# Down projections of two feed-forward nets with one level of Strassen's scheme on two of three token blocks

## The reference, cut to what matters

```python
def swiglu(x, w_gate, w_up, w_down):
    return (jax.nn.silu(x @ w_gate) * (x @ w_up)) @ w_down

    h = x + 0.5 * swiglu(rmsnorm(x, ffn1_norm), ffn1_w_gate, ffn1_w_up, ffn1_w_down)
    ...
    h = h + 0.5 * swiglu(rmsnorm(h, ffn2_norm), ffn2_w_gate, ffn2_w_up, ffn2_w_down)
```

## Time and profile before

| | us |
|---|---|
| median of 3 runs | 1815.75 (1815.69 to 1816.22) |
| the profiled execution | 1815.54 |
| its span, first to last instruction | 1813.7 |
| TensorE busy | 1795.7 |
| VectorE busy | 1030.8 |
| GpSimd busy | 639.2 |
| ScalarE busy | 597.6 |

### The profile page before, as it was taken

One profiled execution on the slowest core, in us unless ns is written; L12 is line 12 of the kernel. 1 busy time (PEld: TensorE's weight loads), 2 busy tenths in 40 slices (PEclk: granted clock), 3 DMA queues, 4 the chain that ended last, 5 costly groups with the idle time before them and its releaser, 6 DMA issues.

```text
span 1813.7 us, 30511 instructions
## 1 busy us (share of the span) xinstructions
PE 1795.7 (99%) x12169; PEld 1783.0 (98%) x12169; DVE 1030.8 (57%) x1726; ACT 597.6 (33%) x1155; POOL 639.2 (35%) x669
## 2 busy tenths in 40 slices
PE   8999999999999999999999999999999999999998
PEld 7999999999999999999999999999999999999998
DVE  6658755554554554823774768555455455544546
ACT  7411322232323233532112455223233323323324
POOL 2687232332333222203994221233233322323321
PEclk9999999999999999999999999999999999999999
DMA  6132111112111111455114501111212111111112
GB/s 171 36 128 101 46 41 53 53 41 60 41 59 48 47 53 39 143 127 123 47 41 125 154 14 53 53 53 43 62 37 60 47 47 53 47 53 48 53 48 94
DMA packets 162494, 119.68 MB, mean 66 GB/s; under 512 B 10242, under 2 KB 156226, under 8 KB 161844
## 3 DMA queue, kind: packets, MB, share of 16 engines
q1 hardware_dynamic: 157012, 110.36, 20.7%
q0 software_dynamic: 864, 5.28, 0.9%
q10 hardware_dynamic: 4480, 2.10, 0.5%
HBM read 102.01 MB, written 15.72 MB: 65 GB/s over the span
## 4 chain that ended last, share of the span: by engine, by line
PE 96%; DVE 2%; ACT 1%; issue 0%; POOL 0%; DVEq 0%; POOLq 0%
PE bank_pair L1004 21%; PE bank_pair L1006 21%; PE bank_pair L1005 21%; PE bank_down L1004 10%; PE bank_down L1006 10%; PE bank_down L1005 10%; DVE HT L2104 1%; DVE XL L2127 1%; PE bank_pair L1387 0%; PE bank_pair L1360 0%; PE bank_pair L1480 0%; PE bank_pair L1379 0%; PE bank_pair L1112 0%; DVE S L2121 0%; PE bank_down L1154 0%
## 5 line engine op out<-in xcount | busy, mean ns | idle before, releaser
L2329 DVE SCALAR_TENSOR_TENSOR HT<-bank_down,HT 128x344 f32<-128x344 f32 (+2 forms) x480 | 246.3, 515 | 369.1 <-PE bank_down L1006 367.1
L1004 PE MATMUL bank_down<-HH,DQH 128*128 128x344 f32 (+2 forms) x924 | 296.0, 320 | 0.0
L1005 PE MATMUL bank_down<-HL,DQH 128*128 128x344 f32 (+2 forms) x924 | 295.0, 319 | 0.0
L1004 PE MATMUL bank_pair<-XHM,U_hi 128*128 128x344 f32 x720 | 230.5, 320 | 1.9 <-issue 1.7
L1006 PE MATMUL bank_pair<-XHM,U_lo 128*128 128x344 f32 x720 | 229.8, 319 | 0.0
L1005 PE MATMUL bank_pair<-XLM,U_hi 128*128 128x344 f32 x720 | 229.5, 319 | 0.0
L2898 POOL TENSOR_TENSOR U_raw<-AST 128x512 f32<-128x512 f32 x36 | 55.1, 1531 | 433.4 <-PE bank_pair L1006 397.4
L1006 PE MATMUL bank_down<-HH,DQ_lo 128*128 128x344 f32 (+2 forms) x624 | 199.7, 320 | 0.0
L1004 PE MATMUL bank_pair<-XH,U_hi 128*128 128x344 f32 x608 | 194.3, 320 | 0.0
L1006 PE MATMUL bank_pair<-XH,U_lo 128*128 128x344 f32 x608 | 194.1, 319 | 0.0
L1005 PE MATMUL bank_pair<-XL,U_hi 128*128 128x344 f32 x608 | 194.0, 319 | 0.0
(11 more groups left out here) (335 smaller groups left out, 3983.8 us busy)
## 6 DMA issues: line engine op xcount, KB each, us to landing
DQ_raw<-in_ffn_w_down SPq DMA_DIRECT2D x52, 256.0 KB, 2.8
U_raw<-in_ffn_w_gate SPq DMA_DIRECT2D x40, 256.0 KB, 3.0
AST<-in_ffn_w_gate SPq DMA_DIRECT2D x40, 256.0 KB, 3.0
U_raw<-in_ffn_w_up SPq DMA_DIRECT2D x40, 256.0 KB, 2.9
AST<-in_ffn_w_up SPq DMA_DIRECT2D x40, 256.0 KB, 3.0
RAW<-in_w_in SPq DMA_DIRECT2D x16, 512.0 KB, 4.5
DQR<-in_ffn_w_down SPq DMA_DIRECT2D x25, 256.0 KB, 2.8
X<-in_x_prompt SPq DMA_DIRECT2D x8, 512.0 KB, 9.0
```

What stands on the lines that cost most here:

```text
L1004: pe.matmul(out, wh, xh, start=first, stop=False, skip_group_check=onto)
L1005: pe.matmul(out, wh, xl, start=False, stop=False, skip_group_check=onto)
L2329: dve.scalar_tensor_tensor(ht, DB[at % 2][:, 0:rows.stop - rows.start], 0.5, ht, ALU.mult, ALU.add).then_inc(pair_free, 1)
```

## The change

For 18 of the 20 pairs (all but the last of each net) the down projection is cut per quarter: 2 output chunks by 2 hidden chunks are the four weight parts A11 to A22, and token blocks 1 and 2 the other operand's columns. They are multiplied by Strassen's scheme (7 products instead of 8), the third token block plainly (4 products). A quarter has nine *steps* (`DOWN_STEPS`): seven with one product (3 matmuls) and two with two (6 matmuls), so 36 steps and 132 matmuls in a pair instead of 24 tiles and 144 matmuls. Some steps accumulate onto what their bank holds (`onto`), after VectorE has added its earlier content to HT; every step is followed by an add (`step_add`, L2499). `STEP_AFTER` issues step n behind chunk 9 + 34n/36: two behind chunks 9 and 26, one behind every other chunk from 10 to 42. New work:

- four sums S1 to S4 of each quarter's weight parts, 128x128 each, on GpSimd (`mix_quarter`, L3149 to L3154, tiles SR), their high parts in one ScalarE operation (`sums_hi`, L1897, tiles SH) and their low parts in one on VectorE (`sums_lo`, L2483, tiles SL); SR and SL share memory, and there are two sets, so a quarter's sums wait for the steps of the quarter two before it
- sums T1 to T4 of hidden blocks on VectorE (`mix_h`, L2520, tiles XTR), with high and low parts (tiles XTH, XTL): nine forms of a pair's hidden blocks instead of six
- the loads of the quarters wait for steps instead of tiles, some counters of small loads at the program's start are merged, and some low parts change their place in VectorE's order.

```diff
+DOWN_STEPS = [((("W", A11, B11),), False, (0, 1)), ((("S", S1, T1),), False, (1, 2)),
+              ((("S", S2, T2),), True, (0, 2)), ((("S", S4, B22),), True, (0, 2)),
+              ((("S", S3, T3),), True, (1, 2)), ((("W", A12, B21),), False, (0, 1)),
+              ((("W", A22, T4),), True, (1, 1)), ((("W", A11, B13), ("W", A12, B23)), False, (0, 0)),
+              ((("W", A21, B13), ("W", A22, B23)), False, (1, 0))]
+STEPS = 4 * len(DOWN_STEPS)
+STEP_AFTER = [9 + 34 * n // STEPS for n in range(STEPS)]
+MIX_BEHIND = [len(DOWN_STEPS) * (q + 1) - 1 for q in range(3)]
+LOWS_BEHIND = [n + 4 for n in MIX_BEHIND]
+BLOCK_OF = {B13: (0, 0), B11: (0, 1), B21: (1, 1), B22: (1, 2), B23: (1, 0)}
+FORMS = [B13, B11, T1, T3, B22, B21, T4, T2, B23]
+PLAIN_FORMS = [B13, B11, T1, T3, B22, B23, B21, T4, T2]
+MIXED = [T3, T1, T2, T4]
+PLAIN_MIXED = [T1, T3, T2, T4]
+
...
+def quarter_end(n):
+
+    p, q = divmod(n, 4)
+    return step_base(p + 1) if p in LAST_PAIR else step_base(p) + len(DOWN_STEPS) * (q + 1)
...
-TILE_AFTER = [5 + 38 * n // TILES for n in range(TILES)]
...
-                    sp.wait_ge(pair_full, 6 * (n - 2))
+                    sp.wait_ge(pair_full, quarter_end(n - 3))
...
+            def bank_of(at):
+
                 if at >= 2:
                     pe.wait_ge(pair_free, at - 1)
                 else:
                     pe.wait_ge(down_free, TILES * (DOWN1 + FO))
+                return DB[at % 2]
+
+            def pair_step(p, n):
+                q, s = divmod(n, len(DOWN_STEPS))
+                parts, onto, _ = DOWN_STEPS[s]
+                k = 4 * p + q
+                pe.wait_ge(dq_ready, k + 1)
+                at = step_base(p) + n
+                out = bank_of(at)[:, 0:TW]
+                for x, (where, unit, form) in enumerate(parts):
+                    if where == "S":
+                        pe.wait_ge(ds_ready, mixed_quarters(k) + 1)
+                    pe.wait_ge(h_split, form_base(p) + forms_of(p).index(form) + 1)
+                    hi, lo = down_part(k, where, unit)
+                    last = product3(out, hi, lo, h_hi_of(p, form), h_lo_of(p, form), x == 0 and not onto,
+                                    x == len(parts) - 1, onto)
+                last.then_inc(pair_full, 1)
+
+            def pair_tile(p, n):
+                tb, j = tile_of(n)
+                q = j // 2
+                pe.wait_ge(dq_ready, 4 * p + q + 1)
...
-                                for n in range(TILES):
-                                    if TILE_AFTER[n] == 4 * i + c:
-                                        pair_tile(p - 1, n)
+                                for n in range(STEPS):
+                                    if STEP_AFTER[n] == 4 * i + c:
+                                        pair_step(p - 1, n)
...
+            def sums_hi(n):
+                act.wait_ge(dq_mixed, 4 * (mixed_quarters(n) + 1))
+                act.activation(SH[n % 2][:, :, :], SR[n % 2][:, :, :], ACT.Copy).then_inc(ds_hi, 1)
...
                         unit_hi(t + 1, A11)
-                        quarter_hi(4 * p - 1)
+                        sums_hi(4 * p - 2)
                         unit_hi(t + 1, A12)
                         copy_sum(t, "M6", (0, 2))
+                        quarter_hi(4 * p - 1)
                         unit_hi(t + 1, S1)
+                        sums_hi(4 * p - 1)
                         copy_sum(t, "M7", (1, 2))
                         unit_hi(t + 1, S2)
...
+                        if p not in LAST_PAIR:
+                            sums_hi(4 * p + 1)
                         h_hi2(p, 0)
...
+            def sums_lo(n):
+                dve.wait_ge(ds_hi, mixed_quarters(n) + 1)
+                dve.tensor_tensor(SL[n % 2][:, :, :], SR[n % 2][:, :, :], f(SH[n % 2][:, :, :]), ALU.subtract
+                                  ).then_inc(ds_ready, 1)
+
+            def quarter_lows(n):
+                if n // 4 not in LAST_PAIR:
+                    sums_lo(n)
+                quarter_lo(n)
+
+            def step_add(p, n):
+                q, s = divmod(n, len(DOWN_STEPS))
+                _, onto, (m, tb) = DOWN_STEPS[s]
+                at = step_base(p) + n
+                dve.wait_ge(pair_full, at + 1)
+                if DOWN_STEPS[s - 1][2] == (m, tb):
+                    dve.wait_ge(pair_free, at)
+                ht = HT[:, 2 * q + m, block_cols(ffn_of(p), tb)]
+                dve.scalar_tensor_tensor(ht, DB[at % 2][:, 0:TW], 0.5, ht, ALU.mult, ALU.add).then_inc(pair_free, 1)
+
+            def mix_h(p, form):
+                e = ffn_of(p)
+                b11, b21, b22 = (h_raw_of(p, x) for x in (B11, B21, B22))
+                b12 = (gated if p in PAIR0 else hidden)(e, (0, 2))
+                raws = 6 * p + 1
+                if form == T1:
+                    dve.wait_ge(h_raw, raws + max(blocks_of(p).index(x) for x in ((0, 1), (0, 2))))
+                    x, y = b12, b11
+                elif form == T3:
+                    dve.wait_ge(h_raw, raws + max(blocks_of(p).index(x) for x in ((1, 2), (0, 2))))
+                    x, y = b22, b12
+                elif form == T2:
+                    dve.wait_ge(h_mixed, mixed_count(p, T1))
+                    dve.wait_ge(h_raw, raws + blocks_of(p).index((1, 2)))
+                    x, y = b22, h_raw_of(p, T1)
+                else:
+                    dve.wait_ge(h_mixed, mixed_count(p, T2))
+                    dve.wait_ge(h_raw, raws + blocks_of(p).index((1, 1)))
+                    x, y = b21, h_raw_of(p, T2)
+                dve.tensor_tensor(h_raw_of(p, form), x, y, ALU.subtract).then_inc(h_mixed, 1)
+
             def pair_add(p, n):
-                tb, j = tile_of(p, n)
-                at = TILES * p + n
...
+                            for n in range(STEPS):
+                                if 4 * i <= STEP_AFTER[n] < 4 * i + 4:
+                                    step_add(p - 1, n)
+                                    if n in LOWS_BEHIND:
+                                        quarter_lows(4 * p - 2 + LOWS_BEHIND.index(n))
+                            if name == "V1b":
+                                unit_lo(t, S2)
+                            if name == "M1":
                                 unit_lo(t, S3)
-                            if t == FIRST[e] + 2 and name == "M2":
...
+                            if p not in LAST_PAIR:
+                                if name == "V2a":
+                                    unit_lo(t + 1, S1)
+                                    unit_lo(t + 1, A11)
+                                if name == "M3":
+                                    c12(t)
+                                    mul_sum(t, "C12", (0, 2))
+                                    mix_h(p, T3)
+                                    mix_h(p, T1)
+                                    h_lo2(p, 1)
+                                    mix_h(p, T2)
+                                    h_lo2(p, 2)
+                                    unit_lo(t + 1, A12)
+                                if name == "M4":
+                                    mul(t, "M4", "x", (1, 1))
+                                    h_lo2(p, 3)
+                                    mix_h(p, T4)
+                                    h_lo2(p, 4)
+                                    h_lo2(p, 5)
+                                if name == "V2b":
+                                    mul(t, "V2b", "y", (1, 0))
+                                    h_lo2(p, 6)
+                                    h_lo2(p, 7)
+                                    h_lo2(p, 8)
+                                continue
                             if name == "V2a":
...
+            def mix_quarter(n):
+                pool.wait_ge(dq_in[QUARTERS[n]], quarter_loads(n))
+                if n >= 2:
+                    pool.wait_ge(pair_full, quarter_end(n - 2))
+                w = quarter(n)[2][:, :].rearrange("p (k m n) -> p k m n", k=2, m=2)
+                s, done = SR[n % 2], 4 * mixed_quarters(n)
+                pool.tensor_tensor(s[:, S1 - S1, :], w[:, 0, 1], w[:, 1, 1], ALU.add).then_inc(dq_mixed, 1)
+                pool.tensor_tensor(s[:, S3 - S1, :], w[:, 0, 0], w[:, 0, 1], ALU.subtract).then_inc(dq_mixed, 1)
+                pool.wait_ge(dq_mixed, done + 1)
+                pool.tensor_tensor(s[:, S2 - S1, :], s[:, S1 - S1, :], w[:, 0, 0], ALU.subtract).then_inc(dq_mixed, 1)
+                pool.wait_ge(dq_mixed, done + 3)
+                pool.tensor_tensor(s[:, S4 - S1, :], w[:, 1, 0], s[:, S2 - S1, :], ALU.subtract).then_inc(dq_mixed, 1)
+
             def ffn_passes(e):
                 for t in range(FIRST[e] + 2, LAST_PASS[e] + 1):
+                    p, g = divmod(t, 2)
+                    if g == 0:
+                        if p - 1 in PAIR0:
+                            mix_quarter(4 * p - 4)
+                        mix_quarter(4 * p - 3)
+                    else:
+                        mix_quarter(4 * p - 2)
+                        mix_quarter(4 * p - 1)
```

(2 more changed lines are left out.)

258 lines of the change are left out of this document (166 added, 92 removed).

## The result

The changed kernel takes **1865.89 us** (median of 4 runs, 1862.17 to 1867.14), the kernel before 1815.83 us on the same chip (4 runs): ratio 1.027, 95% interval 1.025 to 1.029. The profiled execution took 1865.94 us, its span was 1864.1 us.

The account below looks back on a forecast made before the run. TensorE, busy 99% of the span, was taken to bound the kernel. Matmuls removed (-34) and waits at three places (+38, +11, +23) gave +38 us on 1815.5: 1854 us, range 1790 to 1883, likeliest case 1825 to 1875.

Parts of the forecast that it names:

- place 3: Second pass into the next pair: VectorE's added operations delay step 2 by 0.8 or 2.1 us, 16 times; 23 us taken.
- the signs named: Profile signs: 60 to 100 eviction waits, steps 2, 23, 24, 31, 33, GpSimd sums near 0.45 us, 11953 matmuls, pair near 66 us.
- VectorE's wait ahead of c22: Sign in a first pass's middle: VectorE waits about 3 us for ScalarE ahead of sum T (c22).
- What is removed: Down projection quarters, 12 block products to 11: 216 matmuls fewer at 0.1574 us each, 34.0 us saved.
- Place 1: Middle of a pair's first pass: steps 23 and 24 wait 1.2 and 0.85 us, 18 passes, 38 us (29 to 47).
- Place 2: End of a pair's first pass: steps 31 and 33 wait 0.2 and 0.5 us, 16 passes, 11 us (0 to 20).
- The cheap order: At step 2, pass into next pair: S2's low part ends at 471.6, first eviction 472.0, wait 0.8 us.
- the dear one: At step 2, pass into next pair: S2's low part ends at 472.8, first eviction 473.2, wait 2.1 us.
- what stays hidden: First half of the first pass, start of the second pass, and loads: nothing lost; M6 without slack, 8 us with 0.6 us sums.
- TensorE stays fed: Rival, all three places: evictions come in time, the whole 34 us stays, 1782 us; chance 0.22 for the whole case.
- Only the middle costs: Rival: waits only in the first pass's middle, 1819 us, about equal or slower; within 0.2% of before: chance 0.06.
- the contention runs away: Rival: 2.1 us waits at step 2, upper-end middle waits, 0.5 us per second pass; +75 us, 1890 us, chance 0.1.

Follow-up runs that it names:

- the version without waits in its regular pairs: Against the 1788.51 us version with low parts spread: last hidden block's low part (B23) behind step 1's add in the next pass, first pairs excepted; 1783.92 us.
- The run with place 1 moved in full: Against the changed kernel: GpSimd's fourth-quarter sums behind S1 to S3, ScalarE's high part behind S3's, VectorE's two low parts behind step 25; 1825.37 us.
- the move of place 2 alone: Against the changed kernel: next pair's first-quarter sums behind A21's low part, high parts behind A22's, low parts in the second pass; 1882.95 us.
- 1789 us: Against the 1819.02 us version combining three moves of operations: only VectorE's order changed, every low part alone behind one add; 1788.51 us.

## Why the prediction was right or wrong

The direction, the places and most of the prices were right; 1854 was 12 us short of 1866, inside the range. That it came so near is in part luck: 13 us too much at place 3 stand against some 22 that had no term. Of the signs named, the 72 waits, the steps, the sums of 0.46 us, the 11953 matmuls and the 66.2 us of a pair came; VectorE's wait ahead of c22 was 1.93 us and not about 3, and the waits list puts most of the waits down to "issue".

- **What is removed, 34.0 us.** Right: the order's 216 matmuls are gone, and the version without waits in its regular pairs is 32.0 us faster than the kernel before (1815.92 - 1783.92), 34.0 less the 1.5 us of the two first pairs' waits to within 0.5. The spacing of 0.1574 holds in the last row above (62.32 us for the order's 396 matmuls). The 145.8 ns estimated from the Trainium skill (TensorE: Matmul & The Clock Gate, Back-to-back issue gap) is not reached in any stretch that I read.
- **Place 1.** Right to 0.2 us: 1.2 and 0.85 predicted, 1.34 and 0.68 measured, 2.02 without and 2.17 with the refill, 39 us for the 38. GpSimd's sum of 128x128 took 0.46, where I took 0.45. The estimate from the Trainium skill (GPSIMD Engine Reference, Elementwise), 0.28 us, was too short here by 0.18: the time has a part that does not shrink with the width (128x4 took 0.22 us on average). The run with place 1 moved in full was 40.5 us faster than the change, clock and new waits included.
- **Place 2.** Right in sum: 0.2 and 0.5 predicted, 0.22 and 0.33 with 0.08 each behind them measured, 11 us. That step 31 would have cost 1.0 with the sums elsewhere I did not see. In the last pair of each net no sums stand ahead of S4, and step 31 lost 1.09 there; the prediction had left these passes out.
- **Place 3.** The step that failed. I had 0.8 or 2.1 us and took the middle. The cheap order came: VectorE's two low parts follow each other directly, and GpSimd's operation, ready 0.08 us before the second starts, waits for it and lasts 1.89 us (VectorE, then GpSimd in time):

```profile
416.54 0.68 DVE L2474 TENSOR_TENSOR U_lo<-U_raw,U_hi 128x512 fp32r<-128x512 f32 x1
```

```profile
416.46 1.89 POOL L3140 TENSOR_TENSOR U_lo<-AST,U_hi 128x512 fp32r<-128x512 f32 x1 [6.37 <-ACT U_hi L1670]
```

  That is 0.62 us with its refill in 16 passes, 10 us instead of 23. The cheap order's 0.8 us alone would have been 13 us; the weight on the dear one made it 23. But I had priced the first pair of each net at nothing here, without a reason, and there step 2 waited 2.9 us and the clock fell: another 9 us for the two. The two errors nearly cancel.
- **What I left out.** The refill of 0.07 to 0.08 us behind each wait (in the sums above); V1b of the next pair, whose weight part A12 gets its low part at 412.10 to 412.78, 0.24 us in 16 passes, 3.8 us; step 15, 0.16 us in 18, 3.0 us, where I had the first half of the pass among what stays hidden, and the two low parts behind step 12 used a little more than the slack; and the clock, which fell behind steps 23 and 24 in three more pairs, some 5 us. These three make some 11 us. Place 3 with its first pairs came out 4 us below its term, place 1 one above, and step 31 in the last pairs added 2: 10 to 11 of the 12 us. The rest I did not find in the spacings.
- **The rivals.** "TensorE stays fed" did not come, for the reason that stood against it: the chain at place 1 is fixed by the order. Its time, 1782 us, was reached by another order of the same work (1784). "Only the middle costs" and "the contention runs away" are refuted as descriptions of the change: with place 1 moved away 1.95 us a pair were left, and place 3 cost 0.62 us and not 2.1. Places 1 and 3 could be moved away one by one; the move of place 2 alone made a longer wait at the same stretch.

## What to carry to other kernels

When bank reuse leaves an eviction engine some 0.7 us of slack at each step, its busy share says little (64% at 1866 us, 69% at 1789 us): list what can stand ahead of each eviction, and put at most one operation of that length between two of them. A copy or a sum out of PSUM that the evictions stand behind must come ahead of new helper work on every queue in its chain, not only on its own engine. And when one wait has been moved away, read the timeline again before the next step: here the removed sums had been keeping two engines apart.
